# Top-k picked from the score banks, one-hot gate batches spread three to a unit, and fp32r for two attention sums

## The reference, cut to what matters

```python
# mixer: 8 "fox" heads (softmax with a decay) and 8 stick-breaking heads, 128 wide
logits = q @ k.T * HEAD_DIM**-0.5 + c_q[:, None] - c_k[None, :]   # c = cumsum(log_sigmoid(f))
suffix = cumsum(log_1mb, reverse=True) - log_1mb                  # stick-breaking heads
# peer: 8 heads, each with two sets of 128 keys; 128*128 = 16384 experts
q = (xt @ w_pq).reshape(T, 8, 2, 128)
s = einsum('thcd,hcnd->thcn', q, sub_keys)
s1, i1 = top_k(s[:, :, 0], 16);  s2, i2 = top_k(s[:, :, 1], 16)
cand = (s1[..., :, None] + s2[..., None, :])                      # 256 per token and head
top_s, pos = top_k(cand, 16)
idx = (i1 * 128 + i2) at pos;  g = softmax(top_s)
out = sum over the 128 chosen experts of g * gelu(u[idx] . x) * v[idx]
```

## Time and profile before

| | |
|---|---|
| runs, median (lowest to highest) | 3568.72 us (3563.8 to 3572.43), 3 runs |
| the profiled execution's own time | 3573.13 us |
| its span (first to last instruction) | 3571.1 us |
| mean granted clock | 0.982 |
| busy: TensorE, VectorE, ScalarE, GpSimd | 3422.9, 2211.5, 1093.3, 920.0 us |

### The profile page before, as it was taken

The page is one execution under the profiler, slowest core; times in us unless marked ns, Lnnn a source line. Parts: engine busy times, 40 slices in busy tenths (PEclk is TensorE's granted clock), DMA queues, the critical chain, the costliest instruction groups (busy, mean ns, idle before and its releaser), DMA issues.

```text
span 3571.1 us, 43620 instructions
## 1 busy us (share of the span) xinstructions
PE 3422.9 (96%) x16777; PEld 2981.6 (83%) x16777; DVE 2211.5 (62%) x2992; ACT 1093.3 (31%) x1089; POOL 920.0 (26%) x403
## 2 busy tenths in 40 slices
PE   7999999999989987888799999999999999999999
PEld 6777777777878887888789989989999899898887
DVE  4354541112020098988677777777777777778886
ACT  4222323333232223354322223222223222222232
POOL 3333333333433342423211211211212212211000
PEclk9999999999999998999999999999999999999999
DMA  3121222223223333443698888888888988988775
GB/s 141 68 74 70 76 77 71 71 81 118 103 74 112 124 137 129 171 158 134 248 341 308 321 332 309 327 329 307 334 322 308 335 323 311 336 315 318 271 273 209
DMA packets 186274, 755.85 MB, mean 212 GB/s; under 512 B 14049, under 2 KB 104161, under 8 KB 105697
## 3 DMA queue, kind: packets, MB, share of 16 engines
q1 hardware_dynamic: 149344, 486.59, 37.8%
q0 software_dynamic: 36864, 268.45, 20.2%
HBM read 696.27 MB, written 58.72 MB: 211 GB/s over the span
## 4 chain that ended last, share of the span: by engine, by line
PE 57%; issue 25%; DVE 10%; POOL 5%; DMA 2%; ACT 0%; POOLq 0%; SPq 0%; ACTq 0%
PE bank L333 9%; PE bank L335 9%; PE bank L334 9%; PE bank L358 9%; PE bank L356 9%; PE bank L357 9%; POOL wl L319 5%; PE bank L1542 2%; DVE gh L1219 2%; DVE arena L1151 1%; DVE arena L1225 1%; DMA arena<-gate_scratch 1%; DVE arena L1193 1%; DVE arena L1190 1%; DVE arena L1172 1%
## 5 line engine op out<-in xcount | busy, mean ns | idle before, releaser
L333 PE MATMUL bank<-xh,wh 128*128 128x384 f32 (+1 forms) x3184 | 1153.1, 362 | 34.7 <-POOL wl L319 21.7
L335 PE MATMUL bank<-xh,wl 128*128 128x384 f32 (+1 forms) x3184 | 1135.4, 357 | 0.0
L334 PE MATMUL bank<-xl,wh 128*128 128x384 f32 (+1 forms) x3184 | 1134.8, 356 | 0.0
L313 ACT ACTIVATE wh<-raw 128x2048 fp32r<-128x2048 f32 x345 | 659.8, 1912 | 1061.9 <-PE bank L358 542.1
L319 POOL TENSOR_TENSOR wl<-raw,wh 128x2048 fp32r<-128x2048 f32 x126 | 586.5, 4655 | 1129.1 <-ACT wh L313 1129.1
L1255 DVE TENSOR_TENSOR wl<-raw,wh 128x2048 fp32r<-128x2048 f32 x219 | 501.8, 2291 | 321.0 <-ACT wh L313 320.9
L333 PEld LDWEIGHTS bank<-xh,wh 128*128 128x128 f32 x3184 | 605.6, 190 | 84.0 <-POOL wl L319 19.7
L334 PEld LDWEIGHTS bank<-xl,wh 128*128 128x128 f32 x3184 | 604.8, 190 | 45.6 <-issue 1.9
L335 PEld LDWEIGHTS bank<-xh,wl 128*128 128x128 f32 x3184 | 603.4, 190 | 45.7
L356 PE MATMUL bank<-wh,gh 128*128 128x512 f32 x1104 | 429.6, 389 | 1.9 <-DVE wl L1255 1.9
L358 PE MATMUL bank<-wh,gl 128*128 128x512 f32 x1104 | 429.9, 389 | 0.0
(11 more groups left out here) (165 smaller groups left out, 2685.8 us busy)
## 6 DMA issues: line engine op xcount, KB each, us to landing
raw<-in_u SPq DMA_DIRECT2D x128, 1024.0 KB, 5.2
raw<-in_v SPq DMA_DIRECT2D x128, 1024.0 KB, 5.4
raw<-in_w_in SPq DMA_DIRECT2D x57, 1024.0 KB, 4.8
act_scratch<-arena SPq DMA_DIRECT2D x128, 192.0 KB, 3.4
gate_scratch<-arena SPq DMA_DIRECT2D x12, 2048.0 KB, 7.3
arena<-act_scratch SPq DMA_DIRECT2D x32, 768.0 KB, 12.1
arena<-gate_scratch SPq DMA_DIRECT2D x32, 768.0 KB, 15.0
raw<-in_w_out SPq DMA_DIRECT2D x16, 1024.0 KB, 4.8
```

Of the source, the lines that this page charges most:

```text
L313: nc.scalar.activation(wh[s][:], raw[s][:], ACT.Copy).then_inc(hi_done, 1)
L333: nc.tensor.matmul(dst, w_h[:, c], xh[:, c, 0:width], start=(c == 0), stop=False)
L334: nc.tensor.matmul(dst, w_h[:, c], xl[:, c, 0:width], start=False, stop=False)
L335: last = nc.tensor.matmul(dst, w_l[:, c], xh[:, c, 0:width], start=False, stop=(c == KC - 1))
```

## The change

- `first_pick` and `second_pick` take the top-k on VectorE during the query projection, straight from the score banks (all four token blocks of a half-head at once); the stores of the scores to DRAM and their loads go.
- The prologue has 4*11 = 44 units (LAG 11), the main loop 21 groups, the tail 11. The 96 gate batches stand three to a unit in 32 consecutive units, from the 8th unit on. The lookups of token blocks 1 to 3 are quartered and stand behind the one-hots of 12 of these units.
- From the 9th prologue unit on (`LO_DVE`), low parts are made by VectorE.
- In the main loop the gelu writes the activations where the next `v` group takes them, without DRAM; `v` groups are taken in the order 0, 11 to 31, 1 to 10. Groups have 6 and 5 gathered rows in turn instead of 5.
- `cl`, `cr` become fp32r, with high and low parts of the cumulated decay in four strips of 8 partitions; `tri_pe` takes high and low fp32r parts of the first three columns of `sp_`, made by ScalarE and VectorE.

The core of the diff:

```diff
-LAG = 9
+LAG = 11
-TILES0, TILES = 6, 10
-GM = 5
+GATE_FROM = 7
+GATE_STEP = 3
+GATE_UNITS = DB * 32 // GATE_STEP
+LOOK_AT = (None, GATE_FROM, GATE_FROM + 11, GATE_FROM + 22)
+TURN_AT = (GATE_FROM - 1, GATE_FROM + 8, GATE_FROM + 20)
+GM = 6
+LO_DVE = N_PRO + GATE_FROM + 1
...
+            def first_pick(j):
+                h, c, b = j // 2, j % 2, j % 2
+                dve.wait_ge(score_done, j + 1)
+                for tb in range(TB):
+                    last = nc.vector.max(top_v[:, tb, h, c, 0:8], banks[b][:, tb * P:(tb + 1) * P])
+                picked(last)
...
+                last.then_inc(score_out, 1)
...
+            dve.wait_ge(lo_done, LO_DVE)
+            for k in range(GATE_FROM, N_PROUNITS):
+                lo(N_PRO + k + 1)
+                if k < GATE_FROM + GATE_UNITS:
+                    for q in range(GATE_STEP):
+                        hot(GATE_STEP * (k - GATE_FROM) + q)
+                for t in range(1, TB):
+                    if LOOK_AT[t] <= k < LOOK_AT[t] + 4:
+                        lookup(t, (k - LOOK_AT[t]) // 2, (k - LOOK_AT[t]) % 2)
```

ScalarE's program of the prologue:

```diff
+            for k in range(N_PROUNITS):
                 if k:
                     gelu_act(N_PRO + k - 1, M_PRO + k - 1, (k - 1) % 2, k - 1)
                 split_hi(act, N_PRO + k + 1)
+                if k == 3:
+                    act.wait_ge(diff_done, 1)
+                    nc.scalar.activation(weight, weight, ACT.Exp).then_inc(gexp_done, 1)
+                if GATE_FROM < k <= GATE_FROM + GATE_UNITS:
+                    for b in range(GATE_STEP * (k - 1 - GATE_FROM), GATE_STEP * (k - GATE_FROM)):
+                        if b % 8 == 0:
+                            act.wait_ge(gate_stored, 16 * (b // 8 + 1))
+                        act.wait_ge(gate_done, b + 3)
```

TensorE, inside a gate unit, and the suffix sums of `tri_pe`:

```diff
+                    def between(part):
+                        if part in (2, 4, 6):
+                            gate_batch(GATE_STEP * r + part // 2 - 1, i)
...
+                def suffix(j, l):
+                    dst = banks[j][:, (l - j) * P:(TB - j) * P]
+                    if l < SPLIT_COLS:
+                        for part in (sp_hi, sp_lo):
+                            nc.tensor.matmul(dst, neg_tri_r if l == j else neg_ones_r, col_at(part, l),
+                                             start=False, stop=False, skip_group_check=True)
```

VectorE, the decay of a fox head:

```diff
-                nc.vector.tensor_scalar(cl[0:PH], csum, pick, None, ALU.mult)
-                nc.vector.tensor_scalar(cr[32:32 + PH], csum, pick, None, ALU.mult).then_inc(c_ready, 1)
+                nc.vector.tensor_scalar(cl[0:PH], csum_hi.bitcast(F32), pick, None, ALU.mult)
+                nc.vector.tensor_scalar(cl[64:64 + PH], csum, pick, None, ALU.mult)
+                nc.vector.tensor_scalar(cr[32:32 + PH], csum_hi.bitcast(F32), pick, None, ALU.mult)
+                nc.vector.tensor_scalar(cr[96:96 + PH], csum, pick, None, ALU.mult).then_inc(c_ready, 1)
```

ScalarE, the main loop (its loop over the groups is unrolled; `dots_gelu(g)` waits for all dots of its group):

```diff
+                        act.wait_ge(w_lo, g * 4 + (j + 1))
+                        nc.scalar.activation(h_grp[:, j * TD:(j + 1) * TD], gemm_bank[(M_MAIN + j) % 2][:, 0:TD],
+                                             ACT.Gelu).then_inc(freed[(M_MAIN + j) % 2], 1)
                     if k == 4:
-                        dots_gelu(GM, GM, g, 2 * GM)
+                        dots_gelu(g)
...
```

More of the change, by code:

```diff
@@ L86, with group_loads @@
 TURN_AHEAD = 5
[L87 to L94, removed]
+GROUP_SLOTS = []
+for _r in range(NGRP):
+    _s = GROUP_SLOTS[-1].stop if GROUP_SLOTS else 0
+    _n = (GM - _r % 2) if _r < NMAIN else 1 + (_r == NMAIN)
+    GROUP_SLOTS.append(range(_s, _s + _n))
+assert GROUP_SLOTS[-1].stop == SLOTS
+V_ORDER = [0, *range(LAG, NGRP), *range(1, LAG)]
+def group_loads(r):
+    return r + 1 + 1 + max(0, r - NMAIN)
 FOX_OFF = [P * i * (i + 1) // 2 for i in range(TB + 1)]
@@ new lines, in load_gates, with main_sp @@
+            def load_gates(group):
+                sp.dma_start(g_grp.rearrange("p (c n) -> p c n", c=NGC), gate_groups[group]).then_inc(grp_loaded, 16)
+            sp.wait_ge(gate_stored, 16 * NGC + 16)
+            sp.wait_ge(choice_done, 1)
+            load_acts(0)
+            load_gates(V_ORDER[0])
+            load(sp, N_MAIN + 1, u[N_PROUNITS + 1])
+            for k in (N_PROUNITS - 2, N_PROUNITS - 1):
+                store_h(k, M_PRO + k, k % 2)
+            def main_sp(g, v_units, v_next, last):
@@ L763, in softplus_act @@
                 nc.scalar.activation(prob, prob, ACT.Ln, bias=ones[:, 0:1]).then_inc(ln_step, 1)
+                for j in range(SPLIT_COLS):
+                    act.wait_ge(sp_done, s * 8 + 2 * j + 2)
+                    nc.scalar.activation(col_at(sp_hi, j), col_at(sp_, j), ACT.Copy).then_inc(sp_hi_done, 1)
             def weight_act(s):
@@ L1128, in choice_dve @@
[L1128 to L1143 removed]
+            picks = [0]
@@ L1145, in choice_dve, with second_pick @@
+            def second_pick(h):
+                for tb in range(TB):
+                    last = nc.vector.tensor_tensor(
+                        cand[:, tb].rearrange("p (a b) -> p a b", a=TOPK),
+                        top_v[:, tb, h, 0, :].unsqueeze(2).broadcast_to([P, TOPK, TOPK]),
+                        top_v[:, tb, h, 1, :].unsqueeze(1).broadcast_to([P, TOPK, TOPK]), ALU.add)
+                picked(last)
                 for r in range(2):
                     e = slice(8 * r, 8 * r + 8)
-                    for h, c in halves:
-                        last = nc.vector.max(top_v[:, h, c, e], s_of(h, c))
@@ L1204, in choice_dve @@
-                if t is None:
-                    gate_ins.then_inc(gwt_done, 1)
-                    nc.vector.scalar_tensor_tensor(out=g_idx[:], in0=slots[:, 0, :], scalar=float(NKEYS),
-                                                   in1=slots[:, 1, :], op0=ALU.mult,
-                                                   op1=ALU.add).then_inc(chosen_done, 1)
-                    return
-                gate_ins.then_inc(slots_done, 1)
+                    for tb in range(TB):
+                        last = nc.vector.max(best[:, tb, h, e], cand[:, tb])
@@ new lines, in second_pick @@
+                    picked(last)
+                    for tb in range(TB):
+                        last = nc.vector.max_index(pos[:, tb, h, e], best[:, tb, h, e], cand[:, tb])
+                    picked(last)
+                    if r == 0:
+                        for tb in range(TB):
+                            last = nc.vector.match_replace(cand[:, tb], best[:, tb, h, e], cand[:, tb], LOWEST)
+                        picked(last)
+            for h in range(PH):
+                first_pick(2 * h)
+                first_pick(2 * h + 1)
+                second_pick(h)
@@ new lines, in lo @@
+            def lo(k):
+                dve.wait_ge(hi_done, k + 1)
+                nc.vector.tensor_tensor(wl[k % 2][:], raw[k % 2][:], wh[k % 2][:].bitcast(F32),
+                                        ALU.subtract).then_inc(lo_done, 1)
+            for c in range(2):
+                for half in range(2):
+                    lookup(0, c, half)
+            dve.wait_ge(gexp_done, 1)
+            picked(nc.vector.tensor_reduce(gsum[:, 0:TB * PH], weight, AX.X, ALU.add))
+            picked(nc.vector.reciprocal(gsum[:, TB * PH:2 * TB * PH], gsum[:, 0:TB * PH]))
@@ L1349, in _ @@
                 if r == 0:
-                    add_row(NMAIN - 1, 4)
+                    for j in range(4, len(GROUP_SLOTS[NMAIN - 1])):
+                        add_row(NMAIN - 1, j)
                 if r < LAG - 1:
```

509 lines of the change are left out of this document (234 added, 275 removed).

## The result

| | before | after |
|---|---|---|
| median (lowest to highest), 4 runs each | 3569.6 us (3563.8 to 3572.43) | 3592.51 us (3591.73 to 3594.88) |
| span of the profiled execution | 3571.1 us | 3590.6 us |
| mean granted clock | 0.982 | 0.977 |

A forecast was written before the change was run, and what follows sets the result against it. TensorE was taken as the bound: its work in the main loop, its work and waits in the prologue. Prologue +48, attention -12, main loop and tail +4 make +40 us on 3568.7: 3609 us, range 3551 to 3640.

The forecast's parts named there:

- Gate units: Prologue: each of 32 units waits 3.5 us for one-hots at its first batch; 16.1 us a unit including lost clock.
- the clock's part: Prologue: the clock falls to 0.50 behind every one-hot wait, losing 1.55 us each time.
- The start of the prologue: VectorE's leftover picks and lookups before the first token block's slots: 8 us added (0 to 16).
- the wait for slots: Prologue start: by the exclusive-lock rule slots come at about 54 us, TensorE waiting 4 us; by the rows' mean, none.
- Query projection: Top-k from score banks, 19 us a head on VectorE, hides behind TensorE's about 24 us: no cost.
- Attention: Fox and stick-breaking heads together: 12 us gained.
- the logits: Fox heads: the decay's matmul in fp32r takes 0.7 us instead of 2.5 a head; eight heads save 14 us (9 to 18).
- VectorE's two more strips: Fox heads: two more `tensor_scalar` of 0.48 us ahead of the reciprocals lengthen TensorE's wait; 7 us come back.
- more falls: Fox heads: waits of 1.9 us lower the clock more often; 6 us added (-10 to +20).
- The stick-breaking stage: `tri_pe` takes 3.0 us instead of 4.7 a head; seven heads save 12 us, the last loses 1 us.
- Main loop: A sixth gathered row in 11 of 21 groups barely misses a deadline: 4 us added (0 to 25).
- the clock that stays up: Rival, 12%: prologue one-hot waits come but TensorE stays at 2.4 GHz; 50 us less, 3559 us.

The follow-up runs named there:

- Moving the two lines alone: Changed kernel with VectorE making a gate unit's one-hots ahead of the next unit's low part: 3446.15 us, ratio 0.9654 to the kernel before.
- The kernel before with 104 partitions: Kernel before, with the fox heads' fp32 decay matmul taking 104 partitions of cl and cr instead of 40, the added ones zeros: 3555.18 us, ratio 0.9953.

## Why the prediction was right, and where it was not

The direction and the main cause were right; the size was 23 us where 40 were forecast, and most of the difference lies in attention.

- **Gate units: right in mechanism and size.** 32 waits at the first batch, 3.2 us where 3.3 were named for the profile, 16.05 us a unit where 16.1 were summed, 513.7 us in place of 515. Moving the two lines alone took it away. Inside that number the clock's part was wrong in kind: I had it fall every time for 1.55 us; it fell in 22 of 31 units, and each fall cost 1.5 to 2.6 us. The mean, 1.55, agreed by chance.
- **The start of the prologue: the wait for slots mis-sized**, 12.2 us against 4. By the mean of the earlier trace rows there would have been no wait; four steps took 5.4 to 5.6 us, each beside one low part of GpSimd. The exclusive lock for a whole instruction, stated in the Trainium skill, SBUF — State Buffer, section "SBUF: two separate sides", is what the traces show: 5.52 us beside GpSimd in the kernel after, 1.22 us without it. My arithmetic by it fell 8 us short: VectorE had 25 us of picks left at the start of the prologue where I counted 19 (3 us of the pick before, and a second pick of 11.3 us where 9.0 were priced), and seven small operations, 3 us together, stand ahead of the lookups, which I left out. So the slots came at 62.5 us, not at 54. With the clock behind that wait the start cost 14 us (661.6 less 58.5, 513.7 and 75.2) where 8 were added, inside the stated 0 to 16.
- **Query projection: right**, 0.
- **Attention: the step that missed.** -32 us where -12 were summed; almost all of it is the fox heads. At full clock a head went from 56.28 to 54.55 us: the logits save 2.72 us, not 1.8, since 1.2 us of it are the slow change to a 40-partition block and back, which I had not seen in the earlier trace rows, and 1.53 the step to fp32r; VectorE's two more strips give back 0.98 (a wait of 1.94 for 0.96), as priced. Six heads of -1.73 are -10.4 us. The rest is clock: I added 6 us for more falls, but the two of the kernel before, 4.8 us each, became one of 1.6, -8 us. The kernel before with 104 partitions shows both again (-1.18 us a head, no fall). The stick-breaking stage, -12.9 against -11, was right.
- **Main loop: 4 us forecast, 0 measured.** The sixth row in 11 groups made TensorE wait for nothing.

Sum by these steps: +52 - 32 + 0 = +20 us in the span (3590.6 - 3571.1 = 19.5). The 20 us by which attention was missed are the whole difference to the forecast; 4 us too few in the prologue and 4 too many in the main loop cancelled, which was luck. Of the rivals, the clock that stays up came true in 9 of 31 units; in this arrangement it came nearly true altogether at waits of 2.2 us.

## What to carry to other kernels

When an engine makes several things in one program, put what is wanted first ahead of what is wanted last: here a low part with 11 us of slack stood ahead of one-hots with none, and the two lines' order was worth 146 us. Read a wait's length together with the granted clock behind it: here the same wait cost its own length or 1.5 to 2.6 us more, and how often it did could not be told from the length alone. A placement that leaves no wait is safer than one that leaves a short one. A small product is not free of its neighbours: read it from start to start, together with the matmul ahead and its weight load.

## What was not expected of the hardware

- An fp32 weight block of 40 partitions cost 1.2 us in four pairs of small matmuls more than one of 104 partitions with zeros in it (56.28 against 55.10 us a head).
- How often the clock fell behind a wait went from 3 of 31 (2.2 us) over 22 of 31 (3.2 us) to 31 of 31 (4.3 us), while in other arrangements 1.9 us lowered it three times of four and 2.54 us nine of nine; waits of 1.94 us in the fox heads lowered it in one head of six with the fp32r decay and in four of six with the fp32 one.
- Not only two-input operations of VectorE stood still beside a GpSimd low part (5.52 us for 1.22) but a `tensor_scalar` of 8 x 512 too (4.39 for 0.48, as L994 in the earlier trace rows), and GpSimd's low part in its turn beside VectorE's (5.62 for 4.6).
- The clock's falls in one stage changed with edits some 450 us ahead of it: with the suffix sums in fp32, nine of eleven executions took 18 us less than the other two, at a granted clock of 0.981 to 0.984 where those had 0.976 and 0.977; the four of the kernel after all had 0.977. One kernel can go either way: so did the kernel with low parts 4 to 7 by VectorE, once in ten.
